# A two-block transformer kernel: the first result tile read into another slot before the last gate product, and the last normalization turned tile by tile

## The chip, the cores and the metric

The kernel runs on one core of a Trainium2 chip. TensorE (PE) multiplies and transposes, VectorE (DVE) and ScalarE (ACT) do the arithmetic between the products, GpSimd (POOL) computes the powers and starts the indirect transfers, and SyncE (SP) starts nearly every load of weights. The metric is device time in microseconds (us), start to end of one execution; each figure of a run is a median over executions.

## What is computed

Two blocks follow each other on 256 tokens of width 1024, all in float32. The first has two layers, each with attention of several kinds, a merge of branches, and a mixture of 32 experts of which each token takes two. The second has one layer: an input product, branches, a merge, an output product with a norm before it is added to the stream, and a feed-forward part. Cut to what the change touches:

```python
# end of each layer of the first block (l = 0 on 512 tokens, l = 1 on 256)
y = hier_moe(xn2, ...)             # sum over the 2 experts of a token: weight * expert(x)
h = h + gt2 * y
# between the last layer and the second block
x = rms_norm(h, g_final)
h = rmsnorm(x, pre_mix_g[l]);  z = h @ w_in[l]; ...
# middle of the second block
x = x + rmsnorm(merged @ w_mix_out[l], post_mix_g[l])
h = rmsnorm(x, pre_ffn_g[l])
gt = causal_dwconv(h @ w_ff_gate[l], ff_conv_w[l]) + ff_conv_b[l]
y = (gelu(gt) * (h @ w_ff_up[l])) @ w_ff_down[l]
```

## The kernel before, in words

**Tiling.** Tokens stand in tiles of 128: four in layer 0, two from then on. The stream is `h`, tokens by rows. Products need it with features by rows, so each normalized tile is turned by PE (eight 128x128 transposes) and copied out of PSUM into `xT` or `x2T`. PSUM has eight banks: `A` (2), `S` (2), `V` (4). Each has a semaphore `full`, raised by PE, and one `free`, raised by its reader.

**Weights.** SP loads weights in chunks of 2 MB, in the order of a list (`ORDER`), into slots. In the expert part there are eight slots: four of the ring, and four lent by other tensors: slot 4 is `branches[2048:6144]`, slot 5 `heads[2048:6144]`, slot 6 `xT`, slot 7 `values`. A chunk is loaded once the previous chunk of its slot has been read (`last_read`). Expert 31, the last, has its gate weights in slot 5, its up weights in slot 6 and its down weights in slot 7; the last two are loaded in four pieces of 512 KB each (`load_pieces`, L3240). Expert 29's down weights are the last in slot 4. SP's instructions run strictly in their order, and all its transfers share one DMA queue.

**Results of the experts.** The rows of experts 0 to 29 go to memory by indirect transfers that POOL starts (`scatter`, L3054). The last two experts' rows stay in the core (`last_y`) and are added by PE (`last_sum`, L751). `result(l, tile)` (L3280) reads one tile of the rows back, 1 MB. For tile 0 it first waits for all scatters and for the last gate product, `mark["last_gate", l]`, since tile 0 lies in slot 5; as SP's queue is in order, the load of the next stage's weights stands behind that wait. `result_ahead` (L3292) puts each of these reads ahead of a load: tile 0 before U (or v), tile 1 before V (or dv0), tile 2 before VA, tile 3 behind VA and behind the last expert's result (`last_read`).

**The transition between stages.** DVE adds tile 0 in `weigh_first(l, 0)` (L2674), placed between the two halves of the last expert: behind its hidden product (L2575) and before its weighing of the last down product, `last_y[1]` (L2634). PE's `last_sum` needs `last_y[1]`. Behind it PE runs filler products (`keep_going`, L1083, 256 columns with the identity) that keep it busy while DVE, ACT and POOL normalize tile 0; then it turns the tile (L710 in layer 1, L1267 in the second block) and the input products begin (L722, L1299). On POOL, `rows(1)` (L3017) waits for `last_read` and for `y_in[1]`, the landing of tile 1, and then starts five small transfers; ACT's `silu_rows` (L1652) waits for one of them.

**The middle of the second block.** PE runs four output products of 8 x (128x512), tile 0 left and right half, tile 1 left and right half (`out_product`, L1024). ACT squares each, DVE scales and adds (`add_normed`, L2926), ACT squares the sum, DVE forms the normalized tile `x2hat` (L2945). PE runs 20 fillers, and then `norm2_columns` (L1271) turns both tiles: eight rounds of two transposes into `A[0]` and `A[1]` in turn, each copied out by ACT alone (L1937). `feed_forward` (L1516) begins when both banks are empty.

## Time and profile before

| | us |
|---|---|
| runs shown (3): median, lowest, highest | 2712.97, 2710.84, 2713.23 |
| the profiled execution: time | 2711.93 |
| the profiled execution: span, first to last instruction | 2710.1 |
| PE busy | 2493.7 (92% of the span) |
| DVE, ACT, POOL busy | 772.5, 460.6, 170.9 |
| DMA queue of SP | 636.78 MB, 57.4% of 16 engines |
| chain that ended last | PE 74%, DMA 21%, DVE 2%, ACT 2%, issue 2% |

The chain of waits goes back from the last instruction, at each step to what released it. "Issue" is time in which an engine waited for nothing that the profile shows. The profiled execution took 2711.93, its span 2710.1, and 1.83 lies around the span. Three stretches matter here: the transition from layer 0 to layer 1, near 1140 to 1159 us; that from layer 1 to the second block, near 2028 to 2050 us; and the norm between the output product and the feed-forward part, 2432 to 2473 us.

### The profile page before, as it was taken

The numbers are of one execution on the slowest core, as the hardware profiler recorded it, in microseconds if no ns is written. First come the engines' busy times: TensorE is split into PE (matmuls) and PEld (weight loads), VectorE is DVE, ScalarE is ACT, GpSimd is POOL, SyncE is SP. The second block draws the span as 40 slices with busy tenths as digits, with TensorE's granted clock in tenths as the row PEclk, the third lists the DMA queues.
The fourth block names the chain that finished last, engine by engine and source line by source line (L and its number), as shares of the span: only waits on it lengthen the run. The fifth ranks groups of instructions, "written<-read, shape, count | busy, mean of one in ns | idle before, by whom it ended". The sixth has DMA issues, their size and how long they took to land.

```text
span 2710.1 us, 30408 instructions
## 1 busy us (share of the span) xinstructions
PE 2493.7 (92%) x12208; PEld 1524.1 (56%) x12208; DVE 772.5 (29%) x1640; ACT 460.6 (17%) x1039; POOL 170.9 (6%) x195
## 2 busy tenths in 40 slices
PE   8999999999987778799999989777879999999998
PEld 3444554445554444445577655444445688887873
DVE  2694444115311111154343321000002323212210
ACT  2121223101100000022132110000002122102320
POOL 0000000000111111000000011111100000000000
PEclk9999999999999999999999999999999999999999
DMA  8464010424999999964424599999985332344331
GB/s 327 166 241 183 31 63 32 172 108 185 415 425 425 426 426 425 401 240 189 183 94 159 224 425 422 424 426 426 424 372 225 144 125 94 140 155 153 146 142 56
DMA packets 63047, 666.41 MB, mean 246 GB/s; under 512 B 13059, under 2 KB 13347, under 8 KB 24401
## 3 DMA queue, kind: packets, MB, share of 16 engines
q1 hardware_dynamic: 48672, 636.78, 57.4%
q0 software_dynamic: 13392, 24.82, 2.5%
q10 hardware_dynamic: 864, 3.15, 0.3%
q8 instruction: 86, 1.41, 0.2%
q14 instruction: 33, 0.26, 0.0%
HBM read 664.28 MB, written 21.02 MB: 253 GB/s over the span
## 4 chain that ended last, share of the span: by engine, by line
PE 74%; DMA 21%; DVE 2%; issue 2%; ACT 2%; POOL 0%; SPq 0%; DVEq 0%; ACTq 0%; POOLq 0%
DMA ring<-in_w_moe 11%; PE act_bank L733 7%; PE act_bank L722 7%; PE act_bank L852 6%; PE score_bank L1150 5%; PE act_bank L1290 5%; PE vec_bank L868 4%; PE vec_bank L1162 4%; PE vec_bank L1033 4%; PE score_bank L852 3%; PE vec_bank L852 3%; PE act_bank L1527 3%; PE vec_bank L1527 3%; PE vec_bank L1545 3%; DMA xT<-in_w_moe 3%; DMA heads<-in_w_moe 3%
## 5 line engine op out<-in xcount | busy, mean ns | idle before, releaser
L733 PE MATMUL act_bank<-xT,ring 128*128 128x512 f32 (+1 forms) x512 | 193.4, 539 | 0.0
L722 PE MATMUL act_bank<-ring,xT 128*128 128x512 f32 x416 | 183.5, 597 | 2.1 <-DVE xT L2137 1.6
L2575 DVE TENSOR_TENSOR heads<-work,vec_bank 128x256 f32<-128x256 f32 x64 | 27.0, 421 | 505.3 <-PE vec_bank L1150 505.3
L852 PE MATMUL act_bank<-xT,ring 128*128 128x256 f32 (+1 forms) x576 | 157.7, 427 | 1.9 <-issue 1.5
L733 PEld LDWEIGHTS act_bank<-xT,ring 128*128 128x128 f32 x512 | 97.1, 190 | 95.0 <-issue 91.8
L1150 PE MATMUL vec_bank<-ring,branches 128*64 128x256 f32 x1024 | 120.6, 389 | 27.7 <-DMA ring<-in_w_moe 27.7
L1150 PE MATMUL score_bank<-ring,branches 128*64 128x256 f32 x1024 | 122.5, 393 | 23.9 <-issue 12.5
L1162 PE MATMUL vec_bank<-ring,heads 128*64 128x512 f32 x512 | 116.9, 598 | 26.9 <-DMA ring<-in_w_moe 17.4
L852 PEld LDWEIGHTS act_bank<-xT,ring 128*128 128x128 f32 x576 | 109.2, 190 | 44.1 <-issue 32.0
L722 PEld LDWEIGHTS act_bank<-ring,xT 128*128 128x128 f32 x416 | 78.5, 191 | 97.7 <-issue 97.7
L1290 PE MATMUL act_bank<-xT,ring 128*128 128x256 f32 x576 | 126.6, 380 | 0.6 <-ACT work L1943 0.6
L868 PE MATMUL vec_bank<-branches,ring 128*128 128x256 f32 (+1 forms) x416 | 125.6, 445 | 0.0
L1150 PEld LDWEIGHTS score_bank<-ring,branches 128*64 128x64 f32 x1024 | 82.5, 141 | 72.2 <-issue 40.2
L1290 PEld LDWEIGHTS act_bank<-xT,ring 128*128 128x128 f32 x576 | 108.7, 190 | 16.7 <-issue 2.2
L3010 POOL TENSOR_TENSOR stat<-stat,const 128x1 f32<-128x1 f32 (+2 forms) x37 | 24.3, 656 | 1458.5 <-DVE stat L2320 485.8
L1150 PEld LDWEIGHTS vec_bank<-ring,branches 128*64 128x64 f32 x1024 | 77.3, 140 | 68.9 <-DMA ring<-in_w_moe 37.2
L1861 ACT ACTIVATE work<-score_bank 128x256 f32<-128x256 f32 x64 | 24.5, 383 | 516.8 <-PE score_bank L1150 480.3
L1033 PE MATMUL vec_bank<-ring 128*128 128x512 f32 x256 | 111.5, 593 | 0.0
L2157 DVE CUSTOM_DVE_ANT_0 ring<-ring,branches 128x1024 f32<-128x1024 f32 x80 | 100.7, 1280 | 20.6 <-DMA ring<-in_w_ada 20.6
L852 PE MATMUL score_bank<-xT,ring 128*128 128x256 f32 (+1 forms) x320 | 106.1, 472 | 0.0
L3058 POOL DMA_INDIRECT y_rows<-work,table x60 | 60.9, 1015 | 709.4 <-DVE work L2642 680.5
L868 PEld LDWEIGHTS vec_bank<-branches,ring 128*128 128x128 f32 x416 | 79.0, 190 | 38.1 <-issue 30.6
(412 smaller groups left out, 3349.7 us busy)
## 6 DMA issues: line engine op xcount, KB each, us to landing
ring<-in_w_moe SPq DMA_DIRECT2D x96, 2048.0 KB
ring<-in_w_in SPq DMA_DIRECT2D x29, 2048.0 KB
ring<-in_w_merge SPq DMA_DIRECT2D x27, 2048.0 KB
branches<-in_w_moe SPq DMA_DIRECT2D x24, 2048.0 KB
heads<-in_w_moe SPq DMA_DIRECT2D x24, 2048.0 KB
ring<-in_w_ada SPq DMA_DIRECT2D x23, 2048.0 KB
xT<-in_w_moe SPq DMA_DIRECT2D x22, 2048.0 KB
values<-in_w_moe SPq DMA_DIRECT2D x22, 2048.0 KB
```

The lines of the kernel that those rows point to most:

```text
L722: mm = pe.matmul(b.t[:, :], xT[:, k, tile * P:(tile + 1) * P], w[:, k * COLS:(k + 1) * COLS], start=(k == 0), stop=(k == KD - 1))
L733: mm = pe.matmul(b.t[:, 0:n], w[:, k * COLS + f * P:k * COLS + (f + 1) * P], xT[:, k, 0:n], start=(k == 0), stop=(k == KD - 1))
L852: mm = pe.matmul(g.t[:, 0:n], merge_tile(l, i, MERGE_TILES * d + k), xs[:, k, 0:n], start=(k == 0), stop=(k == KD - 1))
L868: mm = pe.matmul(y.t[:, 0:n], merge_tile(l, i, MERGE_TILES * d + KD + k), ys[:, BRANCH_ORDER[i], k, 0:n], start=(k == 0), stop=(k == 3))
L1033: mm = pe.matmul(b.t[:, :], merged[:, k, tile * P:(tile + 1) * P], w[:, k * COLS:(k + 1) * COLS], start=(k == 0), stop=(k == KD - 1))
L1150: mm = pe.matmul(o.t[g * CAP:(g + 1) * CAP, 0:D_HALF], xgT[:, b, c, half * CAP:(half + 1) * CAP], w[:, c0:c0 + D_HALF], start=(k == 0), st ...
L1162: mm = pe.matmul(o.t[g * CAP:(g + 1) * CAP, :], hidT[:, b, c, half * CAP:(half + 1) * CAP], w[:, c0:c0 + HALF], start=(k == 0), stop=(k == 3))
L1290: mm = pe.matmul(b.t[:, 0:SEQ], w[:, k * COLS + f * P:k * COLS + (f + 1) * P], x2T[:, k, :], start=(k == 0), stop=(k == KD - 1))
L1527: mm = pe.matmul(b.t[:, 0:SEQ], ring[s][:, c0:c0 + P], x2T[:, k, :], start=(k == 0), stop=(k == KD - 1))
L1545: mm = pe.matmul(b.t[:, :], hidden[:, k, tile * P:(tile + 1) * P], w[:, c0:c0 + 512], start=(k == 0), stop=(k == FF_TILES - 1))
L2157: ins = nc.vector.tensor_tensor_reduce(ada_junk if k < ns - 1 else w, w, cond_rows[:, k, :], 1.0, bias, ALU.mult, ALU.add, dst)
L3058: pool.indirect_dma_start(out=half_rows(y_rows[l][0:tiles(l) * 2 * P, :]), out_offset=bass.IndirectOffsetOnAxis(ap=table[:, e:e + 1], axis=0),
```

## The change

1. The tiles of the results move: tile 0 from `heads[2048:4096]` (slot 5) to `branches[2048:4096]` (slot 4), tiles 1 and 2 into `heads[2048:4096]` and `heads[4096:6144]`. Tile 0 now waits for the scatters and for expert 29's down product instead of the last gate product; tile 1 takes over the wait for the last gate product.
2. The order on SP's queue changes. Before: tile 0, U, tile 1, V, tile 2, VA, tile 3. After: U, tile 0, V, VA, tiles 1, 2, 3. In the second transition, before: tile 0, v, tile 1, dv0; after: v, tile 0, dv0, tile 1.
3. The last normalization is turned by tile, four transposes into `S[tile]` (copied out by ACT) and four into `V[tile]` (by DVE). Tile 0 is turned between the left and the right output product of tile 1. DVE's copies of tile 0 stand between the two weighings of tile 1 (`between`). The fillers fall from 20 to 12. Of the two functions `turned_mixed` in the diff, the first is ACT's and the second DVE's.

```diff
-    y_tile = [heads[:, 2048:4096], heads[:, 4096:6144], branches[:, 2048:4096], heads[:, 0:2048]]
+    y_tile = [branches[:, 2048:4096], heads[:, 2048:4096], heads[:, 4096:6144], heads[:, 0:2048]]
...
-        def norm2_columns():
+        def turn_mixed(tile):
-            pe.wait_ge(xhat_done.sem, NT * DEPTH + 2 * 2)
-            for f in range(KD):
-                b = A[f % 2]
+            pe.wait_ge(xhat_done.sem, NT * DEPTH + 2 + tile + 1)
+            for q, b in enumerate((S[tile], V[tile])):
                 pe.wait_ge(b.free, b.fills)
-                for j in range(2):
-                    mm = pe.transpose(b.t[:, j * P:(j + 1) * P], x2hat[:, j, f * P:(f + 1) * P], ident)
+                for j in range(4):
+                    f = 4 * q + j
+                    mm = pe.transpose(b.t[:, j * P:(j + 1) * P], x2hat[:, tile, f * P:(f + 1) * P], ident)
                 mm.then_inc(b.full, b.fill())
-            emptied(A[0], A[1])
+                mark["mixed_T", tile, q] = at_bank(b)
...
-        for tile in range(2):
-            for c in range(OUT_CHUNKS):
-                out_product(2, tile, c, 0, KD)
-        pe.wait_ge(V[0].free, V[0].fills)
-        keep_going(20, V[0])
-        norm2_columns()
+        for c in range(OUT_CHUNKS):
+            out_product(2, 0, c, 0, KD)
+        out_product(2, 1, 0, 0, KD)
+        turn_mixed(0)
+        out_product(2, 1, 1, 0, KD)
+        pe.wait_ge(A[1].free, A[1].fills)
+        keep_going(12, A[1])
+        turn_mixed(1)
+        emptied(S[0], S[1], V[0], V[1])
         feed_forward()
...
+        def turned_mixed(tile):
+            b = S[tile]
+            act.wait_ge(*mark["mixed_T", tile, 0])
+            for f in range(4):
+                ins = nc.scalar.activation(x2T[:, f, tile * P:(tile + 1) * P], b.t[:, f * P:(f + 1) * P], ACT.Copy,
+                                           scale=col("pre_ffn_g")[:, f:f + 1])
+            ins.then_inc(b.free, 1)
...
             def weighed(c):
+                if c == 1 and between is not None:
+                    between()
...
+            def turned_mixed(tile):
+                b = V[tile]
+                dve.wait_ge(b.full, b.reads + 1)
+                for j in range(4):
+                    f = 4 + j
+                    ins = TS(x2T[:, f, tile * P:(tile + 1) * P], b.t[:, j * P:(j + 1) * P], col("pre_ffn_g")[:, f:f + 1], None,
+                             ALU.mult)
+                ins.then_inc(b.free, b.read())
+
             for tile in range(2):
-                add_normed(tile, V[2:], mix_g, 0.5)
+                add_normed(tile, V[2:], mix_g, 0.5, (lambda: turned_mixed(0)) if tile else None)
...
+            turned_mixed(1)
...
                 sp.wait_ge(zeroed, 16 * KEPT_EXP * (l + 1))
+                sp.wait_ge(*last_read(max(c for c, s in AT.items() if c[:2] == ("expert", l) and s[0] == NSLOT)))
+            if tile == 1:
                 sp.wait_ge(*mark["last_gate", l])
...
-        result_ahead = {("in", 1, "U"): (0, 0), ("in", 1, "V"): (0, 1), ("in", 1, "VA"): (0, 2),
-                        ("in2", 2, IN2_ORDER[0]): (1, 0), ("in2", 2, IN2_ORDER[1]): (1, 1)}
+        results_behind = {("in", 1, "U"): ((0, 0),), ("in", 1, "VA"): tuple((0, tile) for tile in range(1, NT)),
+                          ("in2", 2, IN2_ORDER[0]): ((1, 0),), ("in2", 2, IN2_ORDER[1]): ((1, 1),)}
+
+        def load_dense(c):
+            load(c)
+            for at in results_behind.get(c, ()):
+                result(*at)
```

## Rows read from the trace of the kernel before

**Rows 1.** Chain of waits, first transition; columns: start us, us, what.

```profile
1139.82 8.60 DMA heads<-y_rows
...
1157.08 0.66 PE score_bank L710 x4
```

**Rows 2.** Chain of waits, second transition.

```profile
2028.13 8.16 DMA heads<-y_rows
...
2038.95 0.70 DVE work L2634
...
2048.21 0.66 PE score_bank L1267 x4
```

**Rows 3.** Timeline of PE: start, duration, instruction, [idle before <-releaser].

```profile
1144.65 3.65 PE L1162 MATMUL vec_bank<-values,heads 128*64 128x512 f32 x16 [0.52 <-issue]
...
1151.89 1.13 PE L759 MATMUL vec_bank<-work 64*128 64x512 f32 x4 [2.53 <-DVE work L2634]
...
2032.96 3.65 PE L1162 MATMUL vec_bank<-values,heads 128*64 128x512 f32 x16 [0.52 <-issue]
...
2039.70 1.13 PE L759 MATMUL vec_bank<-work 64*128 64x512 f32 x4 [2.03 <-DVE work L2634]
```

**Rows 4.** Timeline of SP's DMA queue around the second transition.

```profile
2004.85 5.17 SPq L3246 DMA_DIRECT2D values<-in_w_moe  x1
2010.06 0.43 SPq L3246 DMA_DIRECT2D values<-in_w_moe  x1
...
2029.15 0.43 SPq L3290 DMA_DIRECT2D heads<-y_rows  x1
```

**Rows 5.** DMA issues of windows at 2004.86, 2029.0, 2004.86, 1157.0: KB, us to landing.

```profile
values<-in_w_moe SPq DMA_DIRECT2D x1, 512.0 KB, 27.7
...
heads<-y_rows SPq DMA_DIRECT2D x1, 1024.0 KB, 14.5
...
y_rows<-work,table POOLq DMA_INDIRECT x1, 8.2
...
branches<-in_cond_rows POOLq DMA_DIRECT2D x1, 512.0 KB, 10.6
```

**Rows 6.** Timeline of POOL: the scatter of expert 29, layer 1.

```profile
2007.64 1.01 POOL L3058 DMA_INDIRECT y_rows<-work,table  x1 [13.03 <-DVE work L2642]
```

**Rows 7.** Windows: length, busy by engine, then PE clock, DMA share, GB/s.

```profile
2026.00:2028.00 2.00, 2.00 (x22) 1.61 (x20) 0.00 (x0) 0.00 (x0) 0.00 (x0) 1.00 0.30 119
...
1034.00:1042.00 8.00, 6.28 (x30) 3.89 (x32) 0.00 (x0) 1.19 (x2) 1.03 (x1) 0.53 1.02 428
```

**Rows 8.** Timeline of PE: behind a short and a long wait, and in layer 1.

```profile
2013.93 5.36 PE L1150 MATMUL vec_bank<-ring,branches 128*64 128x256 f32 x32 [2.90 <-DMA ring<-in_w_moe]
...
1034.95 1.09 PE L1213 MATMUL act_bank<-const,work 128*128 128x128 f32 x4 [9.14 <-issue]
...
1171.99 14.00 PE L722 MATMUL act_bank<-ring,xT 128*128 128x512 f32 x32
```

**Rows 9.** Timeline of ACT in the first transition.

```profile
1167.76 1.06 ACT L1655 ACTIVATE branches<-branches 128x1024 f32<-128x1024 f32 x1 [3.38 <-DMA branches<-in_cond_rows]
```

**Rows 10.** Chain of waits from the output product to the feed-forward part.

```profile
2432.22 27.47 PE vec_bank L1033 x64
2459.68 8.63 PE vec_bank L1086 x40
...
2472.43 0.45 issue
2472.88 2.21 PE act_bank L1527 x9
```

**Rows 11.** Timeline of DVE: both normalized tiles, and four copies from PSUM.

```profile
2450.93 0.75 DVE L2945 TENSOR_SCALAR values<-h,stat 128x1024 f32<-128x1024 f32 x1 [0.67 <-POOL stat L3010]
...
2464.67 0.75 DVE L2945 TENSOR_SCALAR values<-h,stat 128x1024 f32<-128x1024 f32 x1 [0.66 <-POOL stat L3010]
...
2049.34 1.13 DVE L2718 TENSOR_SCALAR xT<-vec_bank,cols 128x128 f32<-128x128 f32 x4 [1.19 <-PE vec_bank L1267]
```

More of the change, by code:

```diff
@@ L1935, in second_in @@
             evacuate(A[1], dv[:, 1, 0:COLS])
-        def norm2_columns(gain):
-            for f in range(KD):
-                evacuate(A[f % 2], x2T[:, f, :], ACT.Identity, n=SEQ, scale=col(gain)[:, f:f + 1])
+        def turned_mixed(tile):
[5 more added lines that the diff above has]
+            ins.then_inc(b.free, 1)
         def linear_attention_in():
@@ L2053, in _ @@
                 half_squares(V[2 + c].t[:, :], tile, c, 0.5, *mark["summed", 2, tile, c])
+                if (tile, c) == (1, 0):
+                    turned_mixed(0)
             for c in range(OUT_CHUNKS):
                 half_squares(h[:, tile, c * 512:(c + 1) * 512], tile, c, 1.0, x_done.sem, 2 * tile + c + 1)
-        norm2_columns("pre_ffn_g")
+        turned_mixed(1)
         feed_forward()
@@ L2924, in square_sum, with add_normed @@
             dve.wait_ge(pow_out.sem, pow_in.n)
-        def add_normed(tile, banks, gain, scale):
+        def add_normed(tile, banks, gain, scale, between=None):
             def weighed(c):
+                if c == 1 and between is not None:
+                    between()
                 STT(out=y2[:, tile, c * 512:(c + 1) * 512], in0=banks[c].t[:, :], scalar=scale,
@@ L2946, in mixed_norm @@
                     .then_inc(xhat_done.sem, xhat_done.up())
+            turned_mixed(1)
         def feed_forward():
@@ L3297, in _ @@
                 if c[1] == l and c[0] != "expert" and c not in ORDER[:ADA_FIRST + 2]:
-                    if c in result_ahead:
-                        result(*result_ahead[c])
-                    load(c)
-                    if c == ("in", 1, "VA"):
-                        result(0, NT - 1)
+                    load_dense(c)
                     if c == ("in", 0, "VA"):
@@ L3307, in _ @@
             if c[1] == 2:
-                if c in result_ahead:
-                    result(*result_ahead[c])
-                load(c)
+                load_dense(c)
         for tile in range(2):
```

## The prediction

> **What bounds the kernel now.** I read the page first: PE is busy for 92% of the span and 74% of the chain that ended last is PE, so an edit pays only where the chain leaves PE. Then the chain of waits in order of time, which shows three such places that the change touches.
>
> In the first transition the chain runs through the landing of result tile 0, 1139.82 + 8.60 = 1148.42 [rows 1]. PE has ended the last down product at 1144.65 + 3.65 = 1148.30 and then, but for one small sum, waits for DVE's `last_y[1]` until 1151.89 [rows 3]. The second transition repeats it: the tile lands at 2028.13 + 8.16 = 2036.29, `last_y[1]` starts at 2038.95 [rows 2], the down product ended at 2032.96 + 3.65 = 2036.61, and PE idles 2.03 us [rows 3]. In the norm, the last output product ends at 2432.22 + 27.47 = 2459.69 and the feed-forward part starts at 2472.88, 13.19 later [rows 10].
>
> The third view is the DMA side, because the edit reorders a queue. Landings are counted from the issue. In the second transition the third piece of expert 31's down weights was issued at 2004.85 and took 27.7 [rows 4, 5], so it landed at 2032.55, though SP had put the last piece in the queue by 2010.06 + 0.43 [rows 4]. Tile 0 landed at 2036.29: one piece of 0.5 MB and the tile of 1 MB in 3.74 us, 2.49 us per MB. Tile 1, issued at 2029.15 with 14.5 to landing [rows 4, 5], landed at 2043.65: the load of v (2 MB) and the tile (1 MB) in 7.36 us, 2.45 per MB. The landings are thus spaced as one full queue spaces them, with no gap for the wait of tile 0. Yet at 2026 to 2028 the mean busy share of the 16 DMA engines is only 0.30 [rows 7]. Both hold if a transfer is split over the 16 engines, most of them have finished the pieces, and the slowest still works through a backlog. A transfer lands when its slowest part lands. So what tile 0 waits for is not the instant of its issue but what stands before it on the slowest engine.
>
> **The change, part by part.** *Earlier issue of tile 0.* It needs expert 29's scatter, started at 2007.64 and landed 8.2 later [rows 5, 6], near 2016, against an issue at 2028.13 now. This removes about 12 us from the issue and, by the above, nothing from the landing, for the pieces still end near 2036.29 - 2.45 = 2033.84 on the slowest engine.
>
> *The load of U (or v) now stands ahead of tile 0.* SP is free from 2010.5 [rows 4] and the slot of v held expert 29's up weights, which have been read, so the 2 MB enter the queue before the tile. On the slowest engine they cost 2 x 2.45 = 4.9 us before tile 0: 2041.2 instead of 2036.3. In the first transition likewise 1153.3 instead of 1148.4. The price is nothing if the slowest engine has no backlog, and 4.9 if it has; I take 4.9, by the spacing of the landings. What is queued behind: DVE waits in `weigh_first(l, 0)`, behind it on DVE stands `last_y[1]`, for which PE's second sum waits. All of it moves by 4.9. Loads themselves are not late: U, V and VA come no later than before.
>
> *What comes due next.* Tile 1 in the first transition now stands behind V and VA: on the slowest engine, from 1146.0, U, tile 0, V, VA and tile 1 are 8 MB or 19.6 us, 1165.6, against about 1155.8 now. DVE wants it when tile 0 is normalized, some 5 to 7 us later than before, so it is just in time. POOL's `rows(1)` waits for it too, and behind that are five small transfers. `cond_rows`, issued near 1157, took 10.6 [rows 5] and ACT started on it at 1167.76 [rows 9]. Issued near 1166.4 it lands at 1177.0. ACT then needs 4.4 more until tile 1 is copied (1167.76 to 1172.1 now). PE wants that copy four products into its group of 32 [rows 8], 1171.99 + 4 x 0.44 = 1173.7 now, near 1181.1 with the shift of the next paragraph. So ACT is late by 0.3. If the transfer takes 7 it costs nothing, if it takes 12.5 it costs 2.
>
> *PE's clock.* PE idles 2.53 and 2.03 before `last_sum` [rows 3]; with 4.9 more it idles 7.4 and 6.9. Behind a wait of 2.90, 32 products of 256 columns took 5.36 [rows 8], where 16 of 512, as many columns, take 3.65 [rows 3]: 1.7 lost at the lower level of 1.2 GHz. Behind a wait of 9.14 [rows 8] the mean granted clock of 1034 to 1042 was 0.53 [rows 7], so nearly all of it was at the lower level, until about 6.6 us after PE resumed; work without gaps would lose half of that, 3.3. Both sides bound my case. The fillers and sums behind the wait run without a gap from 1151.89 to 1157.08 in the first transition [rows 1, 3], so the loss is on the path; in the second about 0.3 of it is covered. My waits are nearer 9.14: I take 2.5 and 2.2.
>
> *The norm.* Eight transposes of tile 0 go between two output products. They need `x2hat` of tile 0, written by 2450.93 + 0.75 [rows 11], and PE comes to them at 2432.22 + 3/4 x 27.47 = 2452.82, so they do not wait; they cost 0.9 to 1.1, and I take 1.0. DVE's four copies of tile 0 (1.13 [rows 11]) stand behind the wait for the second squares, ahead of the second weighing, which today just covers POOL's power: they lie on the path, 1.1. They would cost nothing earlier, where DVE idles. `x2hat` of tile 1 was ready at 2464.67 + 0.75 = 2465.42 [rows 11] and comes at 2467.5. The fillers, 8.63 for 20 [rows 10], take 5.2 for 12 and end near 2465.9, so they no longer bind as they did (they ended at 2468.31). PE then idles 1.6, less than the 2.53 behind which no clock fell. From the first transpose to DVE's last copy is 2049.34 + 1.13 - 2048.21 = 2.26 [rows 2, 11] with four banks and two engines. The feed-forward part starts at 2467.5 + 0.1 + 2.3 + the 0.45 of issue [rows 10] = 2470.3, a gain of 2.6. The four rounds of two banks in ACT's tempo go; the gain would be 2.8 at best and 0.9 if the clock fell once (1.7).
>
> **The sum.** 4.9 + 2.5 + 0.3 = +7.7, then 4.9 + 2.2 = +7.1, then -2.6: +12.2 us. Against the profiled execution's 2711.93 that is 2724.1; the median of the runs shown is 1.04 above it, so 2725.2.
>
> **The rivals.** (1) *No engine lags* (the other side: faster). The slowest engine's backlog is that of one execution, or the early load drains it; tile 0 lands by the end of the last down product. Then `last_y[1]` starts at 1148.3 instead of 1151.15 and at 2036.6 instead of 2038.95: -2.8 and -2.3, with the norm -7.7, 2705.3. It gives all of this from the point where the pieces on the slowest engine end 10 us before the down product does (7.4 for load and tile, 2.6 for DVE's two sums); now they end 2.3 and 2.8 before. For it speaks the mean share of 0.30; against it the landings, twice. 14%.
>
> (2) *The tile overtakes the load.* If the parts of tile 0 on the slowest engine complete as before although U is ahead, both transitions stay as they are and the norm alone counts: 2710.4. Against it: v lay between tiles 0 and 1 and tile 1 landed the full 7.36 later [rows 4, 5]. The Trainium skill, "DMA: Bandwidth & Descriptors", section "Queues, rings and completion order", says that completion is not first-in first-out per issuing engine, since later data may be written before earlier data, though each engine takes descriptors in ring order. By the first half of that rule this rival would be open; this trace agrees with the second half, with its 7.36 us. 6%.
>
> (3) *The clock stays up.* Only the 4.9 count: +7.2 with the norm, 2720.2. Against it the 2.90 wait. 8%. (4) *Half the lag:* +2.5 for each transition, 2715.4. 5%. (5) *More than my bounds:* a late small transfer and a long low clock together, over 2731. 3%.
>
> **How the numbers follow.** The forecast has 64%. Its own range, with clock losses of none to 3.3 and 3.0, ACT late by 0 to 2 and the norm at -2.6 to -0.9, is 2720 to 2730. To leave out no more than 2 in 10 the range reaches from 2710 (rivals 2 and 4 are in) to 2731; rivals 1 and 5 are out, 17%. A measurement tells 0.2% from no change, 5.4 us. Faster: rival 1, with a little for a mixture, 0.15. Same, 2707.5 to 2718.4: rivals 2 and 4, 0.11. Slower: the rest, 0.74.
>
> **What would show it.** Right: SP issues U before tile 0, near 1131 and 2011; tile 0 lands near 1153.3 and 2041.2; PE idles about 7 us before `last_sum` and shows a granted clock near 0.5 just after; tile 1 lands near 1165.6; the feed-forward part starts 10.6 us after the last output product, with DVE's copies of tile 0 between POOL's power and the second weighing. Wrong: tile 0 landing before the last down product ends (rival 1), or where it lands now (rival 2); a clock of 1.00 behind a wait of 7 us (rival 3); ACT's first silu more than 2 us behind PE's need.

## The result: slower by 0.4%

| | before | after |
|---|---|---|
| median of 7 runs, us | 2712.77 | 2721.44 |
| lowest and highest | 2710.84 to 2715.67 | 2720.72 to 2728.46 |
| ratio, 95% interval | | 1.004, 1.003 to 1.0049 |
| the profiled execution, us (span) | 2711.93 (2710.1) | 2728.46 (2726.6) |

The change costs 8.7 us by these medians. In a later series beside 21 runs of the kernel before it took 2724.22 against 2712.96, ratio 1.0042 (1.0028 to 1.0055), 11.3 us. The forecast was 2725.2, +12.2.

**The transitions.** The timeline of PE in the profile after (start, duration, instruction, idle before and its releaser), to be laid beside [rows 3]:

```profile
1148.90 3.65 PE L1162 MATMUL vec_bank<-values,heads 128*64 128x512 f32 x16 [0.52 <-issue]
...
1161.14 2.08 PE L759 MATMUL vec_bank<-work 64*128 64x512 f32 x4 [7.53 <-DVE work L2643]
...
1170.42 10.54 PE L722 MATMUL act_bank<-ring,xT 128*128 128x512 f32 x24 [0.57 <-issue]
...
2042.85 3.65 PE L1162 MATMUL vec_bank<-values,heads 128*64 128x512 f32 x16 [0.52 <-issue]
...
2054.98 2.08 PE L759 MATMUL vec_bank<-work 64*128 64x512 f32 x4 [7.41 <-DVE work L2643]
...
2067.26 10.54 PE L1299 MATMUL act_bank<-ring,xT 128*128 128x512 f32 x24 [0.33 <-issue]
```

The waits of 2.53 and 2.03 became 7.53 and 7.41. From the end of the last down product to the first input product it is 1170.42 - 1152.55 = 17.87 and 2067.26 - 2046.50 = 20.76; before, by the same subtraction, 10.43 and 13.01. That is +7.44 and +7.75. The four small products behind each wait take 2.08, where they took 1.13 [rows 3]. The windows of the same profile (columns as in [rows 7]) give a granted clock of 0.53 and 0.50, the lower level of 1.2 GHz:

```profile
1156.00:1166.00 10.00, 4.86 (x10) 2.35 (x10) 4.86 (x7) 1.45 (x4) 0.13 (x1) 0.53 0.97 395
...
2051.00:2060.00 9.00, 5.02 (x12) 2.51 (x12) 4.86 (x7) 1.45 (x4) 0.30 (x1) 0.50 0.87 370
```

SP's queue in the second transition, against [rows 4], and the piece of the chain that follows the tile to its landing in each transition:

```profile
2006.13 14.61 SPq L3267 DMA_DIRECT2D values<-in_w_moe  x4
2020.79 11.12 SPq L3215 DMA_DIRECT2D ring<-in_w_in  x1
2032.08 0.89 SPq L3313 DMA_DIRECT2D branches<-y_rows  x1
```

```profile
1137.89 19.77 DMA branches<-y_rows
...
1157.76 1.30 DVE h L2688
...
1160.40 0.70 DVE work L2643
```

```profile
2032.08 19.49 DMA branches<-y_rows
```

Tile 0 lands at 1157.66, 5.11 behind the end of the last down product (0.12 behind it before), and at 2051.57, 5.07 behind (0.32 ahead of it before). DVE's two sums and `last_y[1]` follow at once, and PE's sum at 1161.14. U, issued at 1135.33 with 19.9 to landing, landed at 1155.2, 2.4 ahead of the tile behind it. The issue of v alone held SP's queue for 11.12.

**The normalization.** Timelines of PE and, in the second fence, of DVE, against [rows 10, 11]:

```profile
2470.29 0.60 PE L1278 MATMUL score_bank<-const,values 128*128 128x128 f32 x4
...
2471.16 7.03 PE L1033 MATMUL vec_bank<-ring 128*128 128x512 f32 x16
2478.03 5.34 PE L1086 MATMUL act_bank<-const 128*128 128x256 f32 x24
2485.02 0.66 PE L1278 MATMUL score_bank<-const,values 128*128 128x128 f32 x4 [1.65 <-DVE values L2965]
...
2487.73 5.39 PE L1527 MATMUL act_bank<-xT,ring 128*128 128x256 f32 x16 [1.61 <-DVE xT L2958]
2492.95 3.62 PE L1527 MATMUL vec_bank<-xT,ring 128*128 128x256 f32 x16
```

```profile
2479.02 0.16 DVE L2930 SCALAR_TENSOR_TENSOR stat<-stat 128x1 f32<-128x1 f32 x1 [7.06 <-ACT work L1910]
2479.10 1.12 DVE L2958 TENSOR_SCALAR xT<-vec_bank,cols 128x128 f32<-128x128 f32 x4
2480.13 0.68 DVE L2940 SCALAR_TENSOR_TENSOR work<-vec_bank,heads 128x512 f32<-128x512 f32 x1
```

From the end of the last output product, 2478.19, the feed-forward part starts 9.54 later instead of 13.19; tile 0's transposes cost 2471.16 - 2470.29 = 0.87 before it. The net is -2.78. But the first sixteen feed-forward products take 5.39, with a granted clock of 0.62 in the window from 2487 to 2490, and the next sixteen 3.62. In the kernel before, the first sixteen took 3.72:

```profile
2472.88 3.72 PE L1527 MATMUL act_bank<-xT,ring 128*128 128x256 f32 x16 [0.96 <-ACT xT L1600]
```

So 1.67 of the 2.78 go back through the lower clock, and the normalization gives 1.1 in this profile.

### The profile page after: what moved, and what is told of

Read it like the earlier page. It is cut to its first block, busy times and chain, and to the rows that moved or that the text cites. A ratio compares the mean times of both kernels' runs of the same rounds, so it can differ in the third digit from the quotient of the medians.

```text
span 2726.6 us, 30386 instructions
## 1 busy us (share of the span) xinstructions
PE 2501.5 (92%) x12192; PEld 1526.1 (56%) x12192; DVE 774.6 (28%) x1648; ACT 460.0 (17%) x1039; POOL 171.0 (6%) x195
## 4 chain that ended last, share of the span: by engine, by line
PE 74%; DMA 19%; SPq 2%; DVE 2%; issue 2%; ACT 1%; POOL 0%; DVEq 0%; ACTq 0%; POOLq 0%
PE act_bank L733 7%; PE act_bank L722 7%; PE act_bank L852 6%; DMA xT<-in_w_moe 5%; PE act_bank L1290 5%; PE score_bank L1150 5%; PE vec_bank L1162 4%; PE vec_bank L868 4%; DMA ring<-in_w_moe 4%; DMA values<-in_w_moe 4%; PE vec_bank L1033 4%; PE score_bank L852 3%; PE vec_bank L852 3%; PE act_bank L1527 3%; PE vec_bank L1527 3%; PE vec_bank L1150 3%
## 5 line engine op out<-in xcount | busy, mean ns | idle before, releaser
L733 PE MATMUL act_bank<-xT,ring 128*128 128x512 f32 (+1 forms) x512 | 194.7, 541 | 0.0
L722 PE MATMUL act_bank<-ring,xT 128*128 128x512 f32 x416 | 184.7, 600 | 2.1 <-DVE xT L2146 1.6
L733 PEld LDWEIGHTS act_bank<-xT,ring 128*128 128x128 f32 x512 | 97.7, 191 | 95.9 <-issue 92.7
L1150 PE MATMUL vec_bank<-ring,branches 128*64 128x256 f32 x1024 | 118.6, 384 | 25.7 <-DMA ring<-in_w_moe 25.7
L1150 PE MATMUL score_bank<-ring,branches 128*64 128x256 f32 x1024 | 119.5, 386 | 24.2 <-issue 12.4
L1162 PE MATMUL vec_bank<-ring,heads 128*64 128x512 f32 x512 | 116.9, 598 | 25.7 <-DMA ring<-in_w_moe 14.4
L722 PEld LDWEIGHTS act_bank<-ring,xT 128*128 128x128 f32 x416 | 79.0, 193 | 98.3 <-issue 98.3
```

The lines of the kernel that those rows point to most:

```text
L722: mm = pe.matmul(b.t[:, :], xT[:, k, tile * P:(tile + 1) * P], w[:, k * COLS:(k + 1) * COLS], start=(k == 0), stop=(k == KD - 1))
L733: mm = pe.matmul(b.t[:, 0:n], w[:, k * COLS + f * P:k * COLS + (f + 1) * P], xT[:, k, 0:n], start=(k == 0), stop=(k == KD - 1))
L1150: mm = pe.matmul(o.t[g * CAP:(g + 1) * CAP, 0:D_HALF], xgT[:, b, c, half * CAP:(half + 1) * CAP], w[:, c0:c0 + D_HALF], start=(k == 0), st ...
L1162: mm = pe.matmul(o.t[g * CAP:(g + 1) * CAP, :], hidT[:, b, c, half * CAP:(half + 1) * CAP], w[:, c0:c0 + HALF], start=(k == 0), stop=(k == 3))
```

## The experiments

All times stand beside runs of the kernel before on the same chip in the same series (medians 2712.39, 2712.96 and 2711.77). The three columns in the middle come from each profile's timeline of PE: from the end of the last down product to the first product at L722, the first input product (A), and to the first at L733, which needs all four tiles (B), both in the first transition, and to the first input product at L1299 in the second (C). Each profile is one execution, so these columns can carry a stretch of lower clock that another execution doesn't have.

| kernel | median, us | ratio, 95% | A | B | C |
|---|---|---|---|---|---|
| before | | | 10.43 | 74.08 | 13.01 |
| after, first profile | 2721.44 | 1.0040 (1.0030 to 1.0049) | 17.87 | 81.52 | 20.76 |
| after_again | 2724.22 | 1.0042 (1.0028 to 1.0055) | 18.04 | 81.69 | 19.14 |
| only_norm | 2710.34 | 0.9999 (0.9990 to 1.0008) | 10.05 | 73.70 | 13.02 |
| only_results | 2726.09 | 1.0050 (1.0036 to 1.0063) | 17.41 | 81.06 | 19.04 |
| tile_ahead | 2717.87 | 1.0017 (1.0008 to 1.0026) | 10.64 | 81.70 | 13.12 |
| tile1_ahead | 2724.53 | 1.0045 (1.0027 to 1.0063) | 17.27 | 80.91 | 20.75 |
| order_before | 2711.60 | 0.9998 (0.9989 to 1.0007) | 11.97 | 75.62 | 14.34 |
| two_loads | 2735.31 | 1.0085 (1.0069 to 1.0102) | 21.66 | 85.30 | 24.75 |
| filled | 2720.70 | 1.0036 (1.0022 to 1.0050) | 16.87 | 80.52 | 18.54 |
| tile_pool | 2714.97 | 1.0012 (1.0003 to 1.0021) | 7.69 | 78.82 | 10.78 |
| pool_in_order | 2706.72 | 0.9979 (0.9970 to 0.9988) | 7.70 | 71.35 | 10.78 |
| pool_in_order_2 | 2706.93 | 0.9982 (0.9973 to 0.9992) | 7.70 | 71.34 | 10.78 |
| pool_kept | 2705.88 | 0.9980 (0.9970 to 0.9989) | 7.70 | 71.35 | 10.78 |

### Each part alone

only_norm is the kernel before with part 3 of the change alone, only_results with parts 1 and 2 alone.

> The kernel before with the change of the last normalization alone. Theory (step 4 of the prediction): 2.6 us less from the last output product to the feed-forward (tile 0's transposes +1.0, the vector engine's copies between the two weighings +1.1, twelve fillers that end before the second weighing is done), with 0.9 to 1.7 us given back if the feed-forward's first products run at the lower clock: 2710.1 to 2711.9 beside a kernel before of 2712.8, ratio 0.9990 to 0.9997. Rival A (the profile of the changed kernel shows the clock low at 2487.5, and that is a property of this ordering): the whole saving but 1 us goes back, 2711.7. Rival B (the normalization gives nothing, and the transitions alone made the +8.7): 2712.8. Rival C: this part costs, over 2713.5.

> The kernel before with the change of the reads of the results alone; the normalization as before. Theory: both transitions lengthen, by 7.44 and 7.75 us in the profile of the changed kernel against the kernel before (last down product to first product of the next stage 17.87 against 10.43, and 20.76 against 13.01), so some 15 us at most, less what the medians took off (the changed kernel's median stands 8.7 over before's, of which the normalization hides 1.1 to 2.8): 2722.5 to 2728, median forecast 2723.5, ratio 1.0036 to 1.0056. Rival: part of the loss came from the normalization or from elsewhere in the expert stage, where the profile of the changed kernel shows three more stretches of lower clock before the first transition: then this kernel stands under 2721.

The reads alone cost 13.7 us, the whole loss and more; the theory holds. The normalization alone took 2.1 less by the medians, but its ratio can't be told from 1. Its profile is the one in which the clock behind the new normalization stayed up:

```profile
2469.38 3.71 PE L1527 MATMUL act_bank<-xT,ring 128*128 128x256 f32 x16 [1.64 <-DVE xT L2958]
```

> The changed kernel itself, beside the next kernels on their chip. The runs so far don't add up: the part of the results alone took 2726.1, the normalization alone 2710.3, the kernel before 2712.4, so both together should take 2724, but the changed kernel's median was 2721.4. If the parts add, it takes 2723 to 2725 here; if something in the combination saves 2 to 3 us, it stays at 2721 to 2722.

The parts add: 2724.2. The 2721.4 of the first series was 0.1% lower, within what the intervals leave open. In the profiles C is 19.14 here and 20.76 in the first one, with less time at the lower clock behind a wait of 7.09.

### The order of SP's queue, put back step by step

`load_dense` of the changed kernel gets a second list, of reads that go ahead of a load. In tile_ahead tile 0 alone moves ahead of U and of v:

```diff
         def load_dense(c):
+            for at in results_ahead.get(c, ()):
+                result(*at)
             load(c)
...
+        results_ahead = {("in", 1, "U"): ((0, 0),), ("in2", 2, IN2_ORDER[0]): ((1, 0),)}
+        results_behind = {("in", 1, "VA"): tuple((0, tile) for tile in range(1, NT)), ("in2", 2, IN2_ORDER[1]): ((1, 1),)}
```

> The changed kernel with one thing undone: tile 0's read is issued ahead of the load of U (first transition) and of v (second), as before, still into the new slot. Theory (2 MB ahead of tile 0 set its landing): tile 0 lands about 4.9 us earlier at each transition than in the changed kernel (at about 1152.8 and 2046.6 by that profile's times), the first part of the sum follows it at once, the wait of TensorE behind the last down product falls from 7.53 and 7.41 to 2.1 to 2.6, and the stretch of lower clock behind it goes; the time is 2710 to 2712. Rival A (what costs is the new slot or tile 1's or tile 0's wait, not the order in the queue): the two waits stay above 7 and the time stays at 2721. Rival B (the landing moves, but the lower clock stays): 2710 + 4.7 = 2715.

The second transition is back (13.12), and with it half of the loss. The first is not: A is back (10.64), B is as long as after (81.70), and so the time is 6 us above my number. The timeline of PE says why:

```profile
1156.12 1.13 PE L759 MATMUL vec_bank<-work 64*128 64x512 f32 x4 [2.75 <-DVE work L2643]
...
1176.45 0.66 PE L710 MATMUL score_bank<-const,values 128*128 128x128 f32 x4 [2.96 <-DVE values L2227]
...
1179.39 3.70 PE L722 MATMUL act_bank<-ring,xT 128*128 128x512 f32 x8
1185.40 12.22 PE L722 MATMUL act_bank<-ring,xT 128*128 128x512 f32 x24 [2.31 <-ACT xT L1672]
...
2049.59 1.13 PE L759 MATMUL vec_bank<-work 64*128 64x512 f32 x4 [2.14 <-DVE work L2643]
```

PE now waits 2.96 for the normalized tile 1 and 2.31 for the copy that ACT makes behind the condition's rows. Twenty-four products then take 12.22 instead of 10.5, 1.7 more. Tile 1 still has V and VA ahead of it. In the kernel after, that was late by as much as tile 0, and hidden behind it.

In order_before the whole order is that of the kernel before, with the new slots and conditions:

```diff
+        results_ahead = {("in", 1, "U"): ((0, 0),), ("in", 1, "V"): ((0, 1),), ("in", 1, "VA"): ((0, 2),),
+                         ("in2", 2, IN2_ORDER[0]): ((1, 0),), ("in2", 2, IN2_ORDER[1]): ((1, 1),)}
+        results_behind = {("in", 1, "VA"): ((0, NT - 1),)}
```

> The changed kernel with the whole order of SyncE's queue as before (tile 0, U, tile 1, V, tile 2, VA, tile 3; tile 0, v, tile 1, dv0), the new slots and the earlier condition of tile 0 kept. Theory, formed from the run with tile 0 alone moved ahead (2717.9; its second transition was back at 13.12 us against 13.01 before, but in the first TensorE waited 2.96 for the normalized tile 1 and 2.31 for the condition's copy): behind the late tile 0 a second lateness was hidden, that of tile 1, which has V and VA ahead of it. With tile 1 back ahead of V, both waits go: down product to the feed-forward's first product near 74 us instead of 81.5, and the time is that of the normalization alone, 2710 to 2711. Rival A (the new slots or the conditions cost something by themselves): 2713 or more. Rival B (the earlier issue of tile 0, 4.6 us earlier, brings something): under 2708.

B is 75.62 and C 14.34, 1.5 and 1.3 above the kernel before, and both times the clock is down behind the wait (first window; columns as in [rows 7]):

```profile
1152.60:1156.00 3.40, 3.40 (x10) 2.13 (x10) 1.68 (x5) 1.45 (x4) 0.56 (x1) 0.54 1.02 434
```

The median can't be told from that of the kernel before, nor from that of only_norm: the slots and conditions cost nothing that these intervals show. Why the clock fell here and not in the kernel before, behind nearly the same waits, stays open. The earlier issue brings nothing:

```profile
2015.26 5.72 SPq L3313 DMA_DIRECT2D branches<-y_rows  x1
```

```profile
2039.12 1.13 PE L759 MATMUL vec_bank<-work 64*128 64x512 f32 x4 [2.24 <-DVE work L2643]
```

Tile 0 was issued 20.6 us ahead of the end of the last down product (2035.81) instead of 8.5, and PE waits 2.24 instead of 2.03. In the first transition it is 17.1 instead of 8.5, and the wait 2.66 instead of 2.53.

In tile1_ahead tile 0 stays behind, and tiles 1 and 2 go ahead:

```diff
+        results_ahead = {("in", 1, "V"): ((0, 1),), ("in", 1, "VA"): ((0, 2),)}
+        results_behind = {("in", 1, "U"): ((0, 0),), ("in", 1, "VA"): ((0, NT - 1),),
                           ("in2", 2, IN2_ORDER[0]): ((1, 0),), ("in2", 2, IN2_ORDER[1]): ((1, 1),)}
```

> The changed kernel with tile 0 left behind U and v, but tiles 1 and 2 ahead of V and VA again. It is the fourth of the orders: both tiles late 81.5 to 81.7 us from the last down product to the first product at L733, tile 0 alone moved ahead 81.7, both moved ahead 75.6 (with one stretch of lower clock in it). Theory (either lateness alone holds the first transition): no gain, tile 0 still sets it: 80.5 to 81.7, and the time of the changed kernel, 2722 to 2725. Rival (what costs in the first transition is tile 1 alone, and tile 0's wait is taken back behind it): 74 to 77 us and 2717 to 2719.

The theory holds: B is 80.91, the time 2724.5. Either tile alone holds the first transition, so that undoing either alone gives next to nothing there.

### Twice the load ahead of tile 0

```diff
-        results_behind = {("in", 1, "U"): ((0, 0),), ("in", 1, "VA"): tuple((0, tile) for tile in range(1, NT)),
-                          ("in2", 2, IN2_ORDER[0]): ((1, 0),), ("in2", 2, IN2_ORDER[1]): ((1, 1),)}
+        results_behind = {("in", 1, "V"): ((0, 0),), ("in", 1, "VA"): tuple((0, tile) for tile in range(1, NT)),
+                          ("in2", 2, IN2_ORDER[1]): ((1, 0), (1, 1))}
```

> The changed kernel with two loads instead of one ahead of tile 0 (U and V; v and dv0). Theory (every load of 2 MB ahead of tile 0 moves its landing by 4.9 us): tile 0 lands 4.9 later still, TensorE's wait behind the last down product grows from 7.1 to 7.6 to about 12.3 at both transitions; tile 1 in the first transition keeps its place in the queue and is no longer what comes next. Down product to input product near 22.9 and 24.5 us instead of 17.9 and 19.6, the whole 2724.2 + 9.8 = 2734. Rival (tile 0 is late because SyncE issues it late or because its parts overtake what is ahead): the landing moves by less than 2 us, 2724 to 2728.

The chain and the timeline of PE:

```profile
1138.00 23.65 DMA branches<-y_rows
```

```profile
2035.41 23.31 DMA branches<-y_rows
```

```profile
1165.13 2.08 PE L759 MATMUL vec_bank<-work 64*128 64x512 f32 x4 [12.47 <-DVE work L2643]
...
2062.13 2.08 PE L759 MATMUL vec_bank<-work 64*128 64x512 f32 x4 [12.44 <-DVE work L2643]
```

The tile lands 10.06 behind the end of the last down product in the first transition (1161.65 - 1151.59) and 10.09 in the second (2058.72 - 2048.63). With no load ahead of it that was 0.12 and -0.32, with one 5.11 and 5.07, with two 10.06 and 10.09: 4.95 to 5.4 for each 2 MB. The issue came only 1.1 and 1.2 us later against that end, so it isn't the issue, and the tile overtook neither load. The time was 2735.3, forecast 2734. A grew by 3.79 only, for the stretch behind the longer wait was the faster one: from the second sum to the input product it is 8.12, and 9.28 in the kernel after.

### What the lower clock costs

In `last_sum` for tile 0, ahead of the rows of the second kept expert:

```diff
+                if n == 1 and fillers:
+                    keep_going(fillers, S[0])
...
-                last_sum(l - 1, 0)
+                last_sum(l - 1, 0, 12)
...
-            last_sum(DEPTH - 1, 0)
+            last_sum(DEPTH - 1, 0, 12)
```

> The changed kernel with twelve more filler products ahead of the second part of the last sum, so that TensorE works through most of the wait for tile 0. Theory (the wait of 7.5 costs about 2.2 to 2.5 at each transition through the lower clock behind it): the tile's landing and the first product's time by the landing stay, the stretch of lower clock behind the wait goes or halves; in the second transition that gives 2.2, in the first only the 1.3 us by which the condition's copy is ahead of TensorE's need in the changed kernel's trace: 3.5 less than the changed kernel, 2 at least. Rival A (the clock is not what these 2.5 us are; the work behind is bound by something else): no gain, the changed kernel's time. Rival B (fillers at the lower clock last past tile 0's landing and hold the sum): slower than the changed kernel.

```profile
1158.14 1.75 PE L761 MATMUL vec_bank<-work 64*128 64x512 f32 x4 [2.17 <-DVE work L2645]
...
2050.48 1.13 PE L761 MATMUL vec_bank<-work 64*128 64x512 f32 x4 [2.17 <-DVE work L2645]
```

The sum starts as long behind the down product as in the kernel after (1158.14 - 1149.52 = 8.62). In the second transition the clock stays up, and from the sum to the input product it is 9.93 us, as before (9.92); in the kernel after it was 12.28, and in the four other profiles with tile 0 behind a load and no such fillers 10.98 to 12.24. In the first transition the clock still falls (1.75 for four products instead of 1.13), and 1.0 of 2.4 is won. The median was 3.5 below the changed kernel's, as forecast, but the two intervals overlap: the trace carries this, not the time.

### Another queue for tile 0

In tile_pool POOL, which starts expert 29's scatter anyway, issues the read of tile 0 as soon as its conditions hold. SP's list loses tile 0 and is otherwise that of the changed kernel.

```diff
+            for b in range(2):
+                pool.wait_ge(scattered[b], 16 * (N_EXP // 2 - 1) * (l + 1))
+            pool.wait_ge(zeroed, 16 * KEPT_EXP * (l + 1))
+            e = N_EXP - KEPT_EXP - 1
+            pool.wait_ge(V[3].full, mark["moe", l]["V"][3] + e // 2 + 1)
+            pool.dma_start(y_tile[0], y_rows[l].rearrange("(t k) n -> t (k n)", k=2)[0:P, :]).then_inc(y_in[0], 16)
...
-            if tile == 0:
+            if tile == 1:
                 for b in range(2):
                     sp.wait_ge(scattered[b], 16 * (N_EXP // 2 - 1) * (l + 1))
...
```

> The changed kernel, but GpSimd issues tile 0's read on a queue of its own, once the scatters, the kept rows' zeroing and expert 29's last down product are done; SyncE's queue keeps its order without it. Theory (tile 0 lands late because of what stands ahead of it on its own queue): with nothing ahead of it, the read lands before the last down product ends, its wait of 7.5 us goes wholly, and both transitions end 2.1 to 2.8 us shorter than before: 2704 to 2708, about 2705.5. Rival A (the sixteen transfer engines serve both queues in the order of issue or share evenly, so that another queue does not overtake): tile 0 lands where it did or halfway, 2715 to 2721. Rival B (the other queue takes from the load of U or v, whose landing then ends last): the wait moves to the first input product, 2708 to 2713. Rival C: GpSimd, which now waits for expert 29's down product ahead of its own work on the condition, is late for the rows of the condition, and the second transition loses what the first wins, 2713 or more.

The DMA issues of the two windows at 1130.7 and 2023 (size, us to landing) and PE's timeline:

```profile
branches<-y_rows POOLq DMA_DIRECT2D x1, 1024.0 KB, 9.3
values<-in_w_moe SPq DMA_DIRECT2D x1, 512.0 KB, 21.8
```

```profile
branches<-y_rows POOLq DMA_DIRECT2D x1, 1024.0 KB, 10.6
```

```profile
1150.48 2.05 PE L759 MATMUL vec_bank<-work 64*128 64x512 f32 x8
...
1173.23 1.12 PE L710 MATMUL score_bank<-const,values 128*128 128x128 f32 x4 [4.45 <-DVE values L2227]
```

Tile 0 lands within 9.3 and 10.6 us, in the midst of a backlog on which SP's own pieces take 21.8, and both waits are gone: A is 7.69, C is 10.78, 2.7 and 2.2 less than before. The issue was early too (19.7 us ahead of the end of the last down product), but that is not the reason: order_before issued the same read 17.1 us ahead of it on SP's queue, behind the pieces, and there it took 17.3:

```profile
branches<-y_rows SPq DMA_DIRECT2D x1, 1024.0 KB, 17.3
```

So it was what stands ahead in its own queue, not the load on the transfer engines as such. The Trainium skill, "DMA: Bandwidth & Descriptors", section "Queues, rings and completion order", says that each transfer engine takes turns between the queues that have work for it; this trace agrees, with 9.3 against 21.8. The median missed my 2705.5 by 9.5. It lies where rival C put it, but not by its mechanism, as the second transition loses nothing: it is tile 1 again, with a wait of 4.45, and B is 78.82.

pool_in_order starts from tile_pool and puts tiles 1 and 2 back ahead of V and VA. It also moves DVE's copies of tile 0 in the last normalization behind the first weighing, with thirteen fillers:

```diff
-        keep_going(12, A[1])
+        keep_going(13, A[1])
...
+        results_ahead = {("in", 1, "V"): ((0, 1),), ("in", 1, "VA"): ((0, 2),), ("in2", 2, IN2_ORDER[1]): ((1, 1),)}
+        results_behind = {("in", 1, "VA"): ((0, NT - 1),)}
...
             def weighed(c):
-                if c == 1 and between is not None:
-                    between()
...
+                if c == 0 and between is not None:
+                    between()
```

> GpSimd issues tile 0's read on its own queue, as in the run before (there tile 0 landed 9.3 and 10.6 us after its issue, well before the last down product ended, and both first waits of TensorE were gone: 7.7 and 10.8 us to the first products against 10.4 and 13.0 before), but tiles 1 and 2 stand ahead of V and VA again; the vector engine's copies of tile 0 in the last normalization move behind the first weighing, with thirteen fillers. Theory (tile 1's place made the 4.7 us that this kernel lost in its first transition): -2.7 and -2.3 at the transitions, -2.6 to -3.9 in the normalization, against the kernel before: 2703.5 to 2705.5. Rival A (with tile 0 out of its way tile 1 or the condition's rows still come too late for TensorE, which is 2.7 us earlier now): the first transition gives 0 to -1, 2706 to 2707.5. Rival B (other stretches of the expert stage slow down because GpSimd waits for a down product): 2710 or more.

With tiles 1 and 2 ahead of V and VA again B falls to 71.35, 2.73 less than before, and no wait for a tile is left there. The kernel is faster than the kernels before and after, 2706.7, though still 1.2 above my range. That is where rival A put it, but not by its mechanism, as the first transition gives its whole 2.7. The copies of DVE behind the first weighing bring the feed-forward part to 8.50 behind the last output product, but in its profile the first sixteen products there take 5.40, so that 1.7 go back. The last expert also gets slower, with PE waiting for its up weights in pieces:

```profile
1144.22 1.08 PE L1150 MATMUL vec_bank<-xT,branches 128*64 128x256 f32 x8 [0.19 <-DMA xT<-in_w_moe]
```

From the start of the down product before the last to the start of the last one it is 14.7 to 16.3 us in the first transition and 13.5 to 13.7 in the second, in the four profiles with the read on POOL's queue; before, it was 13.47 and 12.03. The tile's share of the transfers is the likely price. But three of the profiles without such a read have 13.2 in the second transition too, so how much of it is the tile's isn't shown.

> The kernel in which GpSimd issues tile 0's read and tiles 1 and 2 stand ahead of V and VA, once more, as a partner for the next one: 2706.7, ratio to the kernel before 0.9979, as it was; over 2710 would say that its gain was the chip's or the hour's.

It repeats: 2706.9.

```diff
         turn_mixed(1)
+        keep_going(3, A[1])
         emptied(S[0], S[1], V[0], V[1])
```

> The same with three more filler products between the turning of tile 1 and the feed-forward in the second block, where TensorE idles 1.6 us. In four of the profiles with the new normalization the feed-forward's first sixteen products took 5.3 to 6.4 us instead of 3.7, at the lower clock; in one they did not. Theory (the idle time ahead of the feed-forward brings the clock down, and three fillers of 0.43 cover it without holding anything): 1.6 to 2.7 less than its partner, 2704 to 2705. Rival (it is something earlier, or the fillers delay the feed-forward): no gain, or up to 0.5 slower.

```profile
2463.74 0.66 PE L1278 MATMUL score_bank<-const,values 128*128 128x128 f32 x4 [0.18 <-DVE values L2966]
...
2464.67 1.46 PE L1086 MATMUL act_bank<-const 128*128 128x256 f32 x6
2466.45 3.71 PE L1527 MATMUL act_bank<-xT,ring 128*128 128x256 f32 x16 [0.32 <-issue]
```

With three fillers behind the transposes the feed-forward part starts as early as without them (8.51 behind the last output product, against 8.50) and at full clock: 3.71 instead of 5.40. It is one profile, and that of only_norm shows that the clock can stay up without them; the median fell by 1.05 only, less than the intervals can tell. So this is likely, not shown.

## Why the prediction was right, point by point

**Earlier issue gains nothing: right.** Shown by order_before (20.6 us ahead, wait 2.24) and tile_ahead.

**U or v ahead costs 4.9: right, and the largest term.** Measured from the end of the last down product to the start of the second sum: 8.59 against 3.59 (+5.00) and 8.48 against 3.09 (+5.39). two_loads repeats the price, and tile_pool shows that it belongs to the queue. The 0.30 of mean busy share [rows 7], which spoke for the first rival, didn't count against the spacing of the landings. That it is a mean over engines of which the slowest has a backlog fits this, but the traces don't keep the engines apart: no run shows that one lags, or why. SP came to v as forecast: "near 2011" is 25.6 us ahead of the end of the last down product (2036.61), and in the kernel after SP came to it at 2020.79, 25.7 us ahead (2046.50). What the prediction lacked is that the issue of v holds SP for 11.12. So tile 0 was issued 14.4 us ahead of that end instead of 8.5, 5.9 earlier, and not about 12. It changed nothing, as the issue doesn't set the landing.

**The clock costs 2.5 and 2.2: right in this profile, and in part by luck.** From the second sum to the input product it is 9.28 against 6.84 (+2.44) and 12.28 against 9.92 (+2.36); filled takes the second away. But I had placed my waits between 2.90 and 9.14 as if a longer wait cost more, and that isn't borne out. In after_again, behind waits of 7.55 and 7.09, the same differences are 2.59 and 1.06, in only_results and tile1_ahead 1.8 to 2.3, and in two_loads, behind 12.4, only 1.3 each. The loss differs between executions and doesn't grow with the wait in these profiles.

**ACT late by 0.3: it was in time.** Tile 1 let POOL go on at 1170.53, 21.6 us behind the start of the last down product; I had 20.9. PE needs ACT's copy eight products into its group, not four as I wrote: the row of tile_ahead at 1179.39 that ends there has eight. In the kernel after the copy was ready 1.4 us ahead of that.

**Tile 1 "just in time": right for the sum, and the step that I read too lightly.** In the kernel after, tile 1 costs nothing because tile 0 is as late. The prediction had its landing (1165.6, against 1155.8 before) but drew no rival from it. Had tile 0 been on time, as in rivals 1 and 2, the first transition would have been no shorter: tile_ahead gives 81.70. My 2705.3 and 2710.4 for these cases were therefore too low: the two kernels nearest to them, tile_pool and tile_ahead, took 2715.0 and 2717.9. Two of my expectations for experiments missed by the same oversight.

**The norm -2.6: its parts were right, its clock wrong, and this is the term that failed.** Transposes 0.87 (1.0), DVE's copies between the weighings 1.03 (1.1), PE idle 1.65 (1.6), the net -2.78. The "10.6 after the last output product" counted from where that product ended before, transposes included; so measured it is 10.41. The step that failed is the one that dismissed the clock: "PE then idles 1.6, less than the 2.53 behind which no clock fell". In ten of eleven profiles with this normalization the first sixteen products behind it took 5.3 to 6.6 us instead of 3.7. So 1.6 to 2.9 go back, and the term was -1.1 in the profile of the kernel after and -0.1 in after_again: at my bound of -0.9 or past it. It isn't the sum of the two idle times, of 1.65 and 1.61: in both profiles of pool_in_order the first is down to about 0.2 and the clock falls behind the second, of 1.61, alone. The length of an idle time is thus no bound by itself. What else decides it stays open.

**The sum.** +7.44 +7.75 -2.78 +1.67 = +14.1 in the profile of the kernel after, +13.6 in after_again (7.61 + 6.13 - 2.8 + 2.65), against a forecast of +12.2 and medians of +8.7 and +11.3. The profiled executions stand above the medians of their own kernels (2728.46 against 2721.44, 2725.43 against 2724.22), that of the kernel before stands below its own. The two profiles themselves are 16.5 apart, and 2.45 of that lies outside these terms: the last down product of the first transition ends 4.25 later, and the stretch between the two transitions is 1.80 shorter. What moves single executions by these amounts I did not settle; the stretches of lower clock in the expert stages differ from profile to profile.

The norm gave 1.5 to 2.5 less than its 2.6, and the medians rose by less than the profiles did. The two offset each other, and that the forecast of 2725.2 stands so near the measured 2721.4 and 2724.2 is in part luck. The stated range, from 2710 on, holds the times of rivals 2 and 4 too, so the time alone doesn't decide for this mechanism. The landings and the experiments do.

**The rivals.** No lag and the overtaking: against them order_before and two_loads. The clock stays up: against it the granted 0.53 and 0.50. Half the lag: against it 5.00 and 5.39.

## What to carry to other kernels

On a queue with a backlog the read here landed behind what stood ahead of it, however early it was issued. So price a place in the queue in megabytes (here 2.5 to 2.7 us for each), and look for a second queue before an earlier issue. When an order is changed, list every reader behind it: the latest one hides the next, and undoing half of the order may then give nothing. A short idle time can cost as much again through the clock, as the 1.6 us ahead of the feed-forward part did; in one profile three filler products in it held nothing up.

## What was not expected of the hardware

- A read of 1 MB on POOL's queue landed in 8.7 to 11.6 us (four profiles, two places each), once beside a piece of half its size that took 21.8 on SP's.
- The issue of one 2 MB load held SP for 11.12 us (v, at 2020.79), and that of U in the first transition for 2.39.
- Waits of about the same length bring the clock down or not: the granted clock was 0.54 and 0.56 behind 2.66 and 2.24 us in order_before, and 1.00 behind 2.75 and 2.14 in tile_ahead and behind 2.53 and 2.03 before. In tile_ahead itself it fell behind 2.31 us, at 1185.40, where 24 products took 12.22 instead of 10.54. Behind the 1.61 to 1.64 us ahead of the feed-forward part it fell in ten profiles of eleven.
